# Top-k attention of a two-block model on one core: the fourth tile's multiplication moved to ScalarE, two other steps moved in their queues

## What is computed

```python
score = sum_h relu(q_idx_h . k_idx) * w_h            # which keys a query may use
top_val, top_idx = lax.top_k(score, 128)
logits = q_lat . c_sel * 128 ** -0.5 + rel_bias       # per head
logits = where(valid, logits, -inf)
p = softmax(logits)                                   # exp(x - max) / sum
u = p . c_sel;  o = u . w_uv;  return o @ w_out
```

## Time and profile before

| | us |
|---|---|
| median of three runs | 1999.61 (1997.61 to 2003.10) |
| the profiled execution | 2002.86 |
| its span | 2001.0 |
| PE busy | 1940.7 (97%) |
| DVE busy | 1267.6 (63%) |
| ACT busy | 838.4 (42%) |
| POOL busy | 309.1 (15%) |

### The profile page before, as it was taken

One profiled execution on the slowest core, in us unless ns is written; L12 is line 12 of the kernel. 1 busy time (PEld: TensorE's weight loads), 2 busy tenths in 40 slices (PEclk: granted clock), 3 DMA queues, 4 the chain that ended last, 5 costly groups with the idle time before them and its releaser, 6 DMA issues.

```text
span 2001.0 us, 29796 instructions
## 1 busy us (share of the span) xinstructions
PE 1940.7 (97%) x12273; PEld 1714.6 (86%) x12273; DVE 1267.6 (63%) x1769; ACT 838.4 (42%) x1140; POOL 309.1 (15%) x250
## 2 busy tenths in 40 slices
PE   7999999999999999999999999999997899999998
PEld 5788877789898988999999999999885578889896
DVE  6668766666574754121668476476799658667575
ACT  4438845533142434223454243244534444334243
POOL 2122242200110131021410000002144110000002
PEclk9999999999999999998999999999998999999999
DMA  9844142499999359734265344343121023344351
GB/s 335 217 118 143 71 93 73 177 352 249 227 239 299 122 198 241 162 92 83 85 159 183 118 150 143 114 159 121 70 85 54 22 100 135 129 155 156 102 187 65
DMA packets 68480, 299.14 MB, mean 149 GB/s; under 512 B 6505, under 2 KB 6633, under 8 KB 48386
## 3 DMA queue, kind: packets, MB, share of 16 engines
q1 hardware_dynamic: 38064, 201.15, 28.1%
q0 software_dynamic: 30128, 96.08, 20.2%
q10 hardware_dynamic: 162, 0.10, 0.0%
HBM read 295.19 MB, written 94.96 MB: 195 GB/s over the span
## 4 chain that ended last, share of the span: by engine, by line
PE 62%; issue 23%; DVE 8%; ACT 3%; POOL 3%; DMA 1%; SPq 0%; POOLq 0%; DVEq 0%; ACTq 0%
PE lin L590 36%; PE lin L2048 7%; PE aux L2048 5%; DVE scores L2816 1%; DVE best L2811 1%; PE aux L1613 1%; POOL squares L940 1%; PE aux L2946 1%; PE lin L1568 1%; PE lin L2916 1%; PE aux L2384 1%; ACT w_hi L497 1%; PE aux L2398 1%; DVE scores L2794 1%; DMA w_raw<-in_weights 1%
## 5 line engine op out<-in xcount | busy, mean ns | idle before, releaser
L590 PE MATMUL lin<-x_hi,w_hi 128*128 128x512 f32 (+1 forms) x1128 | 397.1, 352 | 5.4 <-DVE x_lo L2631 2.0
L590 PE MATMUL lin<-x_hi,w_lo 128*128 128x512 f32 (+1 forms) x1128 | 396.0, 351 | 0.0
L590 PE MATMUL lin<-x_lo,w_hi 128*128 128x512 f32 (+1 forms) x1128 | 395.5, 351 | 0.0
L504 DVE TENSOR_TENSOR w_lo<-w_raw,w_hi 128x2048 fp32r<-128x2048 f32 (+1 forms) x101 | 228.8, 2265 | 144.8 <-ACT w_hi L497 144.4
L497 ACT ACTIVATE w_hi<-w_raw 128x2048 fp32r<-128x2048 f32 (+1 forms) x112 | 210.3, 1878 | 204.1 <-PE lin L590 193.1
L590 PEld LDWEIGHTS lin<-x_hi,w_hi 128*128 128x128 f32 x1128 | 211.9, 188 | 38.9 <-issue 4.3
L590 PE MATMUL lin<-v_hi,w_hi 128*128 128x264 f32 (+1 forms) x704 | 237.7, 338 | 6.1 <-DVE tmp L2602 3.5
L590 PEld LDWEIGHTS lin<-x_lo,w_hi 128*128 128x128 f32 x1128 | 212.0, 188 | 29.9 <-issue 0.2
L590 PEld LDWEIGHTS lin<-x_hi,w_lo 128*128 128x128 f32 x1128 | 212.0, 188 | 29.6
L590 PE MATMUL lin<-v_hi,w_lo 128*128 128x264 f32 (+1 forms) x704 | 234.3, 333 | 0.0
L590 PE MATMUL lin<-v_lo,w_hi 128*128 128x264 f32 (+1 forms) x704 | 233.8, 332 | 0.0
(11 more groups left out here) (490 smaller groups left out, 4448.5 us busy)
## 6 DMA issues: line engine op xcount, KB each, us to landing
w_raw<-in_weights SPq DMA_DIRECT2D x112, 1024.0 KB, 4.9
w_raw<-in_weights SPq DMA_DIRECT2D x43, 768.0 KB, 6.1
w_sum<-weight_sums SPq DMA_DIRECT2D x43, 768.0 KB, 4.6
weight_sums<-in_weights POOLq DMA_DIRECT2D x4, 5120.0 KB, 30.9
weight_sums<-in_weights POOLq DMA_DIRECT2D x2, 7168.0 KB, 45.0
w_raw<-weight_sums SPq DMA_DIRECT2D x43, 256.0 KB, 6.2
weight_sums<-in_weights POOLq DMA_DIRECT2D x8, 1280.0 KB, 13.3
weight_sums<-weight_sums POOLq DMA_DIRECT2D x8, 1280.0 KB, 12.8
```

The source lines that it names most:

```text
L504: does.tensor_tensor(w_lo[:, s, 0:n], w_raw[:, s, 0:n], w_hi[:, s, 0:n].bitcast(F32), ALU.subtract).then_inc(sem("w_lo_ready"), 1)
L590: last = nc.tensor.matmul(o, a, b, start=(k % (L.kc // k_banks) == 0 and p == 0), stop=((k + 1) % (L.kc // k_banks) == 0 and p == 2))
```

## The change

- The meta copy of a head (`p_meta_t`) stands ahead of the tile 4 copy on ACT in place of behind it, and its wait for the other copy is gone. `mix` waits for the tile 4 copy as well.
- The multiplication of tile 4 of each head, and of tile 3 of head 0, is an ACT instruction (a copy with a scale per partition) in place of a DVE one; the reciprocal stays on DVE (`share`). DVE announces the maxima and these reciprocals on one semaphore, `at_stats`, in the order of its queue; ACT announces its products on `at_p_act`.
- On DVE normalized(hd+1,2) comes straight behind normalized(hd+1,1), ahead of output_lo(hd-1) and biased(hd+1,4).
- On ACT the product of tile 4 stands behind exp(hd+1,1) and ahead of the copy of tile 3. In head 0, exp(0,4) is moved behind the copies of tiles 1 and 2.

```diff
--- before.py
+++ after.py
@@ -2894,6 +2894,18 @@
                     pool.wait_ge(sem("seen_ready"), 4 * hd)
                     pool_bias_load(pool, hd + 2)
 
+        def by_act(hd, n):
+
+            return hd + 2 if n == 4 else 1 if (hd, n) == (0, 3) else 0
+
+        def max_at(hd, n):
+
+            return 5 * hd + n + (n > 1) if hd else n + (n > 3)
+
+        def share_at(hd, n):
+
+            return 4 if n == 3 else 5 * hd + 7 - (hd == HEADS - 1)
+
         def pe_first_logits(pe):
 
             slot, before, _ = AQ.tile(0, 0, 0)
@@ -2919,7 +2931,10 @@
             def turned(hd, n):
 
                 m = 4 * hd + n - 1
-                pe.wait_ge(sem("at_p"), m + 1)
+                if by_act(hd, n):
+                    pe.wait_ge(sem("at_p_act"), by_act(hd, n))
+                else:
+                    pe.wait_ge(sem("at_p"), 3 * hd + n - min(hd, 1))
                 if m >= 2:
                     pe.wait_ge(sem("at_pt"), m - 1)
                 if hd and n == 1:
@@ -2935,6 +2950,7 @@
                 d = slice(hd * P, hd * P + P)
                 if blocks[0] == 0:
                     pe.wait_ge(sem("at_meta_pt"), hd + 1)
+                    pe.wait_ge(sem("at_pt"), 4 * hd + 4)
                     if hd:
                         pe.wait_ge(sem("at_lo"), hd)
                 for b in blocks:
@@ -2973,7 +2989,7 @@
             mix(HEADS - 1, (0, 1, 2, 3, 4))
 
         def act_exp(act, hd, n):
-            act.wait_ge(sem("at_max"), 4 * hd + n)
+            act.wait_ge(sem("at_stats"), max_at(hd, n))
             t, st = tmp[:, n - 1, 0:KEYS[n]], at_stat[:, n - 1, :]
             nc.scalar.activation(t, t, ACT.Exp, bias=st[:, 1:2], accum_out=st[:, 2:3])\
                 .then_inc(sem("at_exp"), 1)
@@ -2986,26 +3002,33 @@
                 act.wait_ge(sem("at_turned"), 4 * hd + n)
                 if hd >= 2 and n == 1:
                     act.wait_ge(sem("at_o"), hd - 1)
+                if n == 4:
+                    nc.scalar.activation(p_meta_t[:, hd % 2, :], aux[0:META, 3, :], ACT.Copy)\
+                        .then_inc(sem("at_meta_pt"), 1)
                 nc.scalar.activation(p_t[:, hd % 2, 0:n, queries(n)],
                                      aux[:, 1 + n % 2, 0:n * P].rearrange("p (b q) -> p b q", b=n), ACT.Copy)\
                     .then_inc(sem("at_pt"), 1)
-                if n == 4:
-                    act.wait_ge(sem("at_pt"), 4 * hd + 4)
-                    nc.scalar.activation(p_meta_t[:, hd % 2, :], aux[0:META, 3, :], ACT.Copy)\
-                        .then_inc(sem("at_meta_pt"), 1)
 
             def output(hd):
                 act.wait_ge(sem("at_o"), hd + 1)
                 nc.scalar.activation(x_hi[:, hd, 0:S1], aux[:, 0, :], ACT.Copy).then_inc(sem("at_hi"), 1)
 
+            def normalized(hd, n):
+                act.wait_ge(sem("at_stats"), share_at(hd, n))
+                t = tmp[:, n - 1, 0:KEYS[n]]
+                nc.scalar.activation(t, t, ACT.Copy, scale=at_stat[:, n - 1, 3:4]).then_inc(sem("at_p_act"), 1)
+
             exp(0, 3)
-            exp(0, 4)
+            normalized(0, 3)
             for hd in range(HEADS):
                 more = hd + 1 < HEADS
                 turned(hd, 1)
                 turned(hd, 2)
+                if hd == 0:
+                    exp(0, 4)
                 if more:
                     exp(hd + 1, 1)
+                normalized(hd, 4)
                 turned(hd, 3)
                 if more:
                     exp(hd + 1, 2)
@@ -3031,7 +3054,7 @@
                                                as_bank(seen(hd, n), n), ALU.mult, ALU.add)\
                     .then_inc(sem("at_logits_read"), 1)
                 dve.wait_ge(sem("at_logits_read"), m + 1)
-                nc.vector.tensor_reduce(st[:, 1:2], t, AX.X, ALU.max, negate=True).then_inc(sem("at_max"), 1)
+                nc.vector.tensor_reduce(st[:, 1:2], t, AX.X, ALU.max, negate=True).then_inc(sem("at_stats"), 1)
 
             def normalized(hd, n):
                 m = 4 * hd + n - 1
@@ -3040,6 +3063,11 @@
                 link(dve, nc.vector.reciprocal(st[:, 3:4], st[:, 2:3]))
                 nc.vector.tensor_scalar(t, t, st[:, 3:4], None, ALU.mult).then_inc(sem("at_p"), 1)
 
+            def share(hd, n):
+                st = at_stat[:, n - 1, :]
+                dve.wait_ge(sem("at_exp"), 4 * hd + n)
+                nc.vector.reciprocal(st[:, 3:4], st[:, 2:3]).then_inc(sem("at_stats"), 1)
+
             def output_lo(hd):
                 dve.wait_ge(sem("at_hi"), hd + 1)
                 nc.vector.tensor_tensor(x_lo[:, hd, 0:S1], aux[:, 0, :], x_hi[:, hd, 0:S1].bitcast(F32), ALU.subtract)\
@@ -3050,23 +3078,23 @@
                 if n == 4:
                     normalized(0, 1)
                     normalized(0, 2)
+                    share(0, 3)
                 dve_mask(dve, n)
                 dve.wait_ge(sem("masks_ready"), n)
                 link(dve, seen_sum(nc.vector, 0, n))
                 biased(0, n)
             for hd in range(HEADS):
                 more = hd + 1 < HEADS
-                if hd:
-                    normalized(hd, 2)
                 if more:
                     biased(hd + 1, 1)
-                normalized(hd, 3)
+                if hd:
+                    normalized(hd, 3)
+                share(hd, 4)
                 if more:
                     biased(hd + 1, 2)
-                normalized(hd, 4)
-                if more:
                     biased(hd + 1, 3)
                     normalized(hd + 1, 1)
+                    normalized(hd + 1, 2)
                 if hd:
                     output_lo(hd - 1)
                 if more:
```

## The result

| | before | changed |
|---|---|---|
| median of 15 runs each | 2004.95 us | 1995.44 us |
| profiled execution, its span | 2001.0 us | 1993.2 us |
| the attention: TensorE's first logits product behind the last v_all copy, to the first product of AOUT | 74.37 us | 68.03 us |
| from there to the end | 412.84 us | 412.93 us |

The ratio changed to before is 0.9949, 95% interval 0.9938 to 0.9961: faster by 10.2 us (7.8 to 12.4). One execution of the changed kernel took 3830.62 us; it is not in the ratio. The forecast was 10.0 us faster and a time of 1989.6 us (1986.0 to 1994.5). The difference came out right; the time is 0.9 us above the range, because the kernel before took 2004.95 us over 15 runs and not the 1999.61 us of its first three. And the profiles show that one of the three terms of the sum, the start, was wrong, and that the sum lacked a fourth, for the clock.

A forecast was written before the change was run, and what follows sets the result against it. TensorE bounds the kernel, waiting in each head for ScalarE's meta copy and VectorE's product of tile 2. Steady part 5.8, start 2.4 and end 1.8 us sum to 10.0, so 1999.6 - 10.0 = 1989.6 us (1986.0 to 1994.5).

The forecast's parts named there:

- the start: Head 0 to transposes 3 of head 1: waits before transposes 4 and 2 shrink, 2.4 us gained (1.3 to 3.5).
- I forecast the median, 1999.6 - 10.0: Whole kernel: median of 1989.6 us, from a base of 1999.6 us less a gain of 10.0 us.
- The steady part: Heads 1 to 6: five periods going from 8.51 to 7.35 us (7.25 to 7.6), 5.8 us gained (4.5 to 6.3).
- The floor of 7.22: Each steady head: TensorE's own time if both its waits go, 7.22 us.
- The term for GpSimd's added collisions: Steady heads: POOL's shifted sums may fall on DVE's products of tiles 1 and 2; 0.08 us a head (0 to 0.3).
- The end: Head 7: transposes 2's wait of 1.18 us and the meta copy's 0.6 go; 1.8 us gained (1.5 to 1.95).
- DVE's product of tile 3 may then be last, held by two POOL sums: Transposes 3 of head 1: 0.1 us taken off the 2.5 us gained there.
- Rival (c): Heads 0 and 1: clock low longer or longer DVE wait reaches PE; gains 0.5 us or less, 1991.5; chance 0.12.
- (b): Heads: a new ring through ACT is slower; with table reloads 8.9 us, 2003.6 us or more in all; chance 0.03.
- (a): Heads: DVE and POOL set the period, colliding at tiles 1, 2 and 3; 7.7 us, 1992.1 in all; chance 0.17.
- (d): Steady heads: an overlooked in-order wait holds PE at over 7.9 us a head; about 1994.6 us; chance 0.11.
- the ring in the prediction: Each head: tile 4's logits (PE), its bias and maximum (DVE), tile 2's product (DVE), tile 2's transposes (PE); 0.48 us wait.

The follow-up runs named there:

- third_on_act: Changed kernel with tile 3's product on ScalarE in all heads; attention 62.90 us, ratio to before 0.9940.
- after_again: Changed kernel again, no edit, for a second profile and ratio; attention 63.47 us, ratio to before 0.9955.
- pool_later: Changed kernel with GpSimd's sums for head 3 held until tile 2 of head 2 is biased; attention 64.38 us, ratio to before 0.9937.
- third_and_end: third_on_act with mix waiting for the tile 4 copy only ahead of block 1; attention 62.70 us, ratio to before 0.9922.
- meta_and_second: Kernel before with meta copy first and tile 2's product sooner, no products on ScalarE; attention 67.43 us, ratio to before 0.9960.
- null_before: Kernel before, unchanged, against itself; attention 77.74 us, ratio 0.9995.
- act_only: Changed kernel with meta copy and tile 2's product back in their old places; attention 80.72 us, one execution of 2007.86 us.
- exp04_back: Changed kernel with exp(0,4) back ahead of the copies of head 0; attention 67.46 us, ratio to before 0.9948.

## Why the prediction was right in the difference and wrong in the time

- **The base.** "I forecast the median, 1999.6 - 10.0": the step that failed. Three runs (1997.61 to 2003.10) stood for the kernel, and each case got 1.5 us of spread. The 74 executions of the kernel before in the experiments have a mean of 2004.9 and go from 1997.2 to 2013.8. They sort by their mean granted clock: 1997.8 us at 0.994 (8 runs), 2002.5 at 0.991 (12), 2007.4 at 0.988 (11), 2010.3 at 0.986 (10). The first three all lie below the mean. In the 14 profiles of this case the stage starts between 1510.2 and 1514.7, and what lies behind it takes 412.8 to 413.1. If that holds for the executions without a profile, some 12 of the 16.6 us between the extremes arise in the attention itself; no profile of a long execution of before is there to show it. With a base of 2004.95 the forecast would have been 1994.95.
- **The steady part.** Said 5 x 1.16 = 5.8 us; 42.57 - 37.17 = 5.4 from transposes 4 of head 1 to those of head 6. The floor of 7.22 was right (7.24 in third_on_act). The term for GpSimd's added collisions, 0.08 a head, measured 0.19 in heads 3 and 4, where GpSimd's sum of 144 columns comes right behind the issue of a bias DMA (7.43 against 7.24), and 0 in the later ones. In head 2 the half clock is in the period too: 7.82 from transposes 4 to transposes 4, over the 7.6 of the bound. It did hit tile 1's product (0.62 for 0.29 us), as the prediction had it.
- **The end.** Said 1.8 us; 13.09 - 11.23 = 1.86. The wait at the last mix stayed, 1.20 us for about 1.2.
- **The start.** Said +2.4 us (1.3 to 3.5); from the stage's start to transposes 4 of head 1 the first pair of profiles gives 18.71 - 19.63 = -0.9, and after_again 18.71 - 14.78 = +3.9. Neither lies within the bounds. "DVE's product of tile 3 may then be last, held by two POOL sums", for 0.1 us, was the step: it was held by three, for 1.9 us, and behind the wait that this made came a stretch of half clock, to 1534. The prediction had named that as a sign of being wrong: "a clock below 1.00 after 1530". Up to transposes 2 of head 1 the changed kernel was 13.86 - 10.47 = 3.4 us ahead; 2.0 went to the product, 2.3 to the clock. pool_later removes the product's part by an edit. That the clock fell because of this wait is likely and not shown by itself: after_again, pool_later, third_on_act and third_and_end, without the wait, have no such stretch in head 1, but the waits of 1.79 us in head 1 of before and of 2.02 us in head 0 of the changed kernel had none behind them either. Rival (c) had "the clock stays low longer" but with another cause. Where the race is won the start gives more than I claimed, since there the clock is also up from head 0 on.
- **The missing term.** The sum took a wait at its length. The clock was priced in heads 0 and 1 only. At equal mean clock the two kernels differ by 8.0 us (2002.5 and 1994.5 at 0.991), 7.7 (2007.4 and 1999.7 at 0.988), 7.6 at 0.990 and 10.1 at 0.992. The changed kernel's 22 runs have a mean clock of 0.9910, the 74 of before 0.9895 (the difference is three times its standard error), and by the slope within before (1547 us for a clock of 1) that is another 2.3 us. So of the 10.4 us between the means, by this estimate, about 8 are waits and overlap and 2.3 are clock. That the sum came to 10.0 is in part luck: 0.4 too much in the steady part and up to 3.3 too much at the start against the first profile, and 2.3 of clock not counted.
- **Rivals.** (b), the ring through ScalarE, did not show: no table load, no wait for ScalarE's product in heads 1 to 7; adding a second product per head there cost nothing. (a), VectorE and GpSimd as the bound, holds for meta_and_second (7.50 to 7.96) and in a small way for heads 3 and 4 of the changed kernel (7.43). (d) did not come.
- **The rule against it.** The Trainium skill, "ScalarE: Activation LUTs", Rules for kernel authors, puts a multiplication on VectorE and not on ScalarE. For a product alone the traces agree: 0.735 us on ScalarE against 0.50 on VectorE. But beside GpSimd's sums the same product took VectorE 1.10 us, and with it there a head lasted about 0.3 us longer (meta_and_second).
- **The parts together.** In us a head: meta copy first alone 8.51 (10.20 where the clock fell), second product sooner alone 7.87, both 7.50 to 7.96, both with the product on ScalarE 7.24 to 7.44 in heads 3 to 5; that product alone 8.52. The meta copy is worth something only once the second product is sooner, as the ring in the prediction had it.

## What to carry to other kernels

A wait of TensorE, where it is the bound, can cost more than its length, since the clock sometimes falls behind it; look at the granted clock of many executions before taking a few runs as the base, and give the range the spread of that clock. When one engine holds another up, a step that starts 0.1 us behind the other's row of work can pay for several steps of it (2.32 us for 0.43): find which of them can be held back, or put the step on a third engine. Take a ring apart in all its places at once; half of the edit can be worth nothing, or less.

## What the runs showed of the hardware

- With a wait of TensorE of 1.11 us in each 8.51 us the granted clock fell from 1.00 to 0.50 for part of every head from 2 on in one of two profiles, and 8 of 12 further executions had a time and a mean clock close to that profile's; with waits of 0.50 and 0.48 us apart, in the same 8.51 us, it fell in no head from 2 to 6 of three profiles (before, null_before, act_only). With 0.7 us of work put into the first, the long executions were gone. Whether the clock falls behind a given wait varies: behind the last wait of 1.20 us it stayed at 1.00 in the changed kernel and fell to 0.50 in exp04_back.
- A one-input product on VectorE that started beside a GpSimd sum ended, in nearly all cases, shortly behind that sum or behind a later one of the same row: by 0.10 us with 144 columns, 0.17 with 272, 0.22 with 400 and 0.30 with 528. The product of 400 took 0.89 us for 0.43 with one sum and 2.32 with three in a row. Biases that read PSUM and reductions kept their length beside the same sums (tile 1's maximum 0.30 us).
- A ScalarE copy of 528 columns with a scale per partition takes 0.735 us, like the exponential of the same shape (0.73), and behind it the next starts after 0.62 to 0.64.
